# Making the low parts of two streamed weight slabs in one VectorE operation, in a two-block transformer kernel on one core

## The reference, cut to what matters

```python
h = rmsnorm(x, norm_g);  (... q, k, v, gates ...) = split_cols(h @ w_in, IN_SIZES)
merged = g_a * (oa @ w_up_a) + g_b * (ob @ w_up_b) + g_c * (oc @ w_up_c)
x = x + merged @ w_o
proj = rms_norm(h, g_pre_mix) @ w_in_2
m = sigmoid(gate_a) * (pool(proj) @ w_pool_out) + sigmoid(gate_b) * (conv(proj) @ w_conv_out)
h = h + rms_norm(m @ w_o_2, g_post_mix)
f = square(relu(rms_norm(h, g_pre_mlp) @ w_up_2)) @ w_down_2
h = h + rms_norm(f, g_post_mlp)
```

## Time and profile before

| | before |
|---|---|
| runs shown (3) | 2047.82, 2048.43, 2048.82 us |
| median | 2048.43 us |
| profiled execution, span from first to last instruction | 2046.3 us |
| own time of the profiled execution | not listed apart from its span |
| TensorE busy | 2034.2 us, 99% |
| TensorE weight loads | 1732.4 us, 85% |
| VectorE busy | 1358.7 us, 66% |
| ScalarE busy | 948.2 us, 46% |
| GpSimd busy | 80.7 us, 4% |
| low parts by rows, L487 | 438 operations, 540.2 us |
| DMA | 389.23 MB, mean 190 GB/s |

### The profile page before, as it was taken

The page is one execution under the profiler, slowest core; times in us unless marked ns, Lnnn a source line. Parts: engine busy times, 40 slices in busy tenths (PEclk is TensorE's granted clock), DMA queues, the critical chain, the costliest instruction groups (busy, mean ns, idle before and its releaser), DMA issues.

```text
span 2046.3 us, 29256 instructions
## 1 busy us (share of the span) xinstructions
PE 2034.2 (99%) x10572; PEld 1732.4 (85%) x10572; DVE 1358.7 (66%) x1815; ACT 948.2 (46%) x1225; POOL 80.7 (4%) x91
## 2 busy tenths in 40 slices
PE   9999999999999999999999999999999999999998
PEld 7888898888888888999888888888888888888886
DVE  6766756576756565678999756576556556645655
ACT  6645444565544444433444644553333333333343
POOL 0000102001011000002000000000000000000001
PEclk9999999999999999999999999999999999999999
DMA  9687555555566555555666565655565565555652
GB/s 348 196 199 189 176 155 182 183 168 180 185 217 220 192 188 187 171 175 158 193 194 200 181 232 185 196 171 189 194 189 185 194 195 181 196 191 184 194 195 103
DMA packets 265468, 389.23 MB, mean 190 GB/s; under 512 B 12504, under 2 KB 147032, under 8 KB 264571
## 3 DMA queue, kind: packets, MB, share of 16 engines
q1 hardware_dynamic: 262587, 377.19, 57.7%
q0 software_dynamic: 2624, 10.54, 2.0%
q10 hardware_dynamic: 144, 0.01, 0.0%
HBM read 385.02 MB, written 2.54 MB: 189 GB/s over the span
## 4 chain that ended last, share of the span: by engine, by line
PE 98%; SPq 1%; DMA 1%; DVE 0%; ACT 0%; issue 0%; DVEq 0%
PE acc L607 19%; PE acc L609 19%; PE acc L608 19%; PE acc L630 18%; PE acc L628 10%; PE acc L622 2%; PE acc L620 2%; PE acc L621 2%; PE acc L626 1%; PE aux L1489 1%; PE aux L1573 1%; DMA stage_rows<-in_w_mem_kv 1%; PE aux L1503 0%; PE acc L546 0%; PE acc L545 0%; PE acc L544 0%
## 5 line engine op out<-in xcount | busy, mean ns | idle before, releaser
L487 DVE TENSOR_TENSOR low_rows<-stage_rows,high_rows 128x1024 fp32r<-128x1024 f32 x438 | 540.2, 1237 | 404.1 <-ACT high_rows L476 399.2
L476 ACT ACTIVATE high_rows<-stage_rows 128x1024 fp32r<-128x1024 f32 x438 | 462.3, 1059 | 581.7 <-PE acc L609 531.0
L487 DVE TENSOR_TENSOR w_low<-stage,w_high 128x1024 fp32r<-128x1024 f32 (+1 forms) x264 | 320.7, 1221 | 230.8 <-ACT w_high L476 226.3
L476 ACT ACTIVATE w_high<-stage 128x1024 fp32r<-128x1024 f32 (+1 forms) x264 | 276.2, 1047 | 417.0 <-PE acc L630 298.9
L630 PE MATMUL acc<-u,w_high 128*128 128x512 f32 x900 | 247.9, 394 | 0.0
L607 PE MATMUL acc<-high_rows,f_pair 128*128 128x512 f32 x496 | 193.0, 389 | 0.0
L608 PE MATMUL acc<-low_rows,f_pair 128*128 128x512 f32 x496 | 192.9, 389 | 0.0
L609 PE MATMUL acc<-high_rows,f_pair 128*128 128x512 f32 x496 | 192.9, 389 | 0.0
L630 PE MATMUL acc<-hT,w_high 128*128 128x512 f32 x645 | 177.5, 394 | 0.0
L630 PEld LDWEIGHTS acc<-u,w_high 128*128 128x128 f32 x900 | 152.9, 189 | 19.0
L628 PEld LDWEIGHTS acc<-u,w_low 128*128 128x128 f32 x960 | 146.8, 188 | 20.6
(11 more groups left out here) (409 smaller groups left out, 3348.0 us busy)
## 6 DMA issues: line engine op xcount, KB each, us to landing
stage_rows<-in_w_in SPq DMA_DIRECT2D x160, 512.0 KB, 3.6
stage<-in_w_in SPq DMA_DIRECT2D x136, 512.0 KB, 3.5
stage_rows<-in_w_down SPq DMA_DIRECT2D x128, 512.0 KB, 4.3
stage<-in_w_up SPq DMA_DIRECT2D x120, 512.0 KB, 3.9
stage_rows<-in_w_o SPq DMA_DIRECT2D x64, 512.0 KB, 3.6
stage_rows<-in_w_pool_out SPq DMA_DIRECT2D x16, 512.0 KB, 3.8
stage_rows<-in_w_conv_out SPq DMA_DIRECT2D x16, 512.0 KB, 4.5
stage_rows<-in_w_mem_kv SPq DMA_DIRECT2D x14, 512.0 KB, 11.6
```

The source lines that it names most:

```text
L476: act.activation(high[:, pr, 0:kt, 0:p.cols], src[:, slot, 0:kt, 0:p.cols], ACT.Copy).then_inc(high_done, 1)
L487: dve.tensor_tensor(low[:, pr, 0:kt, 0:p.cols], src[:, slot, 0:kt, 0:p.cols], high[:, pr, 0:kt, 0:p.cols].bitcast(F32), ALU.subtract).then ...
```

## The change

Two helpers and a branch come into subtract_low. `two_tiles` says whether a slab is by rows with two tiles and not one of the first four of w_up_first. `in_couple` says whether slab n and its neighbour (n even: n+1, n odd: n-1) are both so. For a slab in such a couple the call for the even one issues nothing, and the call for the odd one waits until both are rounded and makes both low parts in one operation over two neighbouring places of each ring, 2048 columns. It then adds 2 to split_done. All others are made as before. ScalarE's rounding, the loads and TensorE's program are unchanged.

```diff
+        def two_tiles(n):
+
+            job, _, idx = stream_of_slabs[n]
+            p, _, _, kt, _ = job.pieces[idx]
+            return p.by_rows and kt == 2 and not (job is jobs["w_up_first"] and idx < 4)
+
+        def in_couple(n):
+
+            first = n - n % 2
+            return isinstance(n, int) and first + 1 < len(stream_of_slabs) and two_tiles(first) and two_tiles(first + 1)
+
         def subtract_low(dve, job, i, u, idx):
             n, n_static = job.slab(i, u, idx)
             p, _, k, kt, _ = job.pieces[idx]
             slot, pr = n_static % STAGES, n_static % PAIRS
+            if isinstance(n, int) and in_couple(n):
+                if n % 2:
+                    dve.wait_ge(high_done, n + 1)
+                    dve.tensor_tensor(low_rows[:, pr - 1:pr + 1], stage_rows[:, slot - 1:slot + 1],
+                                      high_rows[:, pr - 1:pr + 1].bitcast(F32), ALU.subtract).then_inc(split_done, 2)
+                return
             dve.wait_ge(high_done, n + 1)
```

## The result

| | before | after |
|---|---|---|
| runs | 2047.82 to 2048.82, four runs | 2059.78, 2060.67, 2062.17, 2064.82 |
| median | 2048.3 us | 2061.42 us |
| ratio, 95% interval | | 1.0067 [1.0054, 1.0080] |
| span of the profiled execution | 2046.3 us | 2057.7 us (its own time: 2059.78) |

The medians are 13.1 us apart.

The account below looks back on a forecast made before the run. TensorE, busy 2034.2 of 2046.3 us, was taken as the bound. mem_kv +3.6 and conv_gates with pool_out +4.2 gave +7.8 us, forecast 2056.2 us; the range ran from 2052.0 less 0.2 to 2064.

Parts of the forecast that it names:

- the 7 to 10 foretold: Sign expected in the changed kernel's profile: TensorE's waits for L487 low parts come to 7 to 10 us in all.
- The operation: VectorE's merged 2048-column operation takes 2294 ns; 209 couples save 180 ns each, 38 us busy time, priced at nothing.
- The spare time: Steady stages: the even slab's spare time before TensorE wants it falls from 5.6 to 1.7 us; nothing is lost.
- mem_kv: Term for the start: late couples (2, 3) and (8, 9) cost +3.6 us, the largest delay standing, not the sum.
- The first delay: In mem_kv, couple (2, 3) makes TensorE start slab 2 at 15.5 instead of 13.12: 2.4 us.
- the second delay: In mem_kv, couple (8, 9) makes slab 9 start at 37.25 instead of 33.46: 3.8 us for everything behind.
- Similar sums for w_up_a and w_up_c come out within half a us of nothing: Low-part readiness against TensorE's start in w_up_a and w_up_c: loss within half a us of nothing, left out.
- conv_gates and pool_out: Term of +4.2 us: delays add up, 0.7 at 338, 0.7 at 356, 1.8 at 390, 1.0 at 324.
- rival 2: TensorE's clock falls in one or both stalls at the start; two falls cost +4, about 2060 us; chance 0.10.
- Rival 1: Only the start is paid, TensorE not waiting at 338, 356 and 390: +3.6 us, 2052.0; chance 0.12.
- Rival 3: VectorE's backlog bites fully in conv_gates and pool_out, plus 2 us in w_down3: +15, about 2063 us; chance 0.18.
- Rivals 4 and 5: TensorE gains in conv_gates, at most 4 us, chance 0.03; the change does nothing anywhere, chance 0.01.

Follow-up runs that it names:

- experiments 3: Changed kernel with couples only in the steady stages (w_o, conv_out, w_o_2 and the w_down jobs; 98 couples): 2048.10 us, ratio 1.0001.
- 12: Changed kernel with 180 couples: none in mem_kv, at 320 to 334, 384 to 398, or at 156, 162, 208, 230, 338, 356; 2048.33 us.
- experiment 7: Couples only in the steady stages, plus an unused 1024-column subtraction ahead of each of 45 couples in w_down0 to w_down2: 2049.25 us, ratio 1.0007.
- experiment 8: Couples only in the steady stages, plus an unused 2048-column subtraction ahead of each of 45 couples in w_down0 to w_down2: 2071.31 us, ratio 1.0113.
- experiment 1: Changed kernel with couples in mem_kv alone (7 of the 209): 2051.02 us, ratio 1.0015.
- experiment 5: Changed kernel without couples in mem_kv, and in w_up_b the body runs ahead of the couple on VectorE: 2056.67 us, ratio 1.0042.
- Experiment 10: Changed kernel without couples in mem_kv, and with slabs 388 and 389 split singly: 2055.95 us, ratio 1.0039.
- 6: Changed kernel without couples in mem_kv, with 26 unused transposes on TensorE before its wait for slab 390: 2057.74 us, ratio 1.0046.
- 4: Changed kernel, but at the odd slab two operations of 1024 columns, each adding 1, in place of one of 2048: 2053.99 us, ratio 1.0028.
- 2: Changed kernel with all couples but those of mem_kv (202 of them): 2058.74 us, ratio 1.0054.
- 9: Changed kernel without couples in mem_kv and at eleven places late or one couple ahead of a late one (191 left): 2050.54 us, ratio 1.0013.
- 11: Changed kernel with 28 unused transposes on TensorE before its wait for slab 2: 2061.09 us, ratio 1.0065.

## Why the prediction was right, and where its sizes were off

Direction, mechanism and range held: slower, because the even slab's low part waits for the odd slab, at places where the spare time is short. Predicted +7.8 us, measured +11.4 in the span and +13.1 in the median. That the waits for low parts come to 8.3 us, within the 7 to 10 foretold, is in part luck: the forecast has two stalls of 2.7 us in mem_kv, the trace one of 3.7, and 2.9 at slab 390 where it has 1.8. Step by step:

- **The operation** (2.29 us, 209 couples, worth nothing): 2.31 us, 209, and by experiments 3 and 12 worth nothing. VectorE's busy time fell by 28 us to 1330.7 and not by 38; 209 x (2 x 1237 - 2308) ns is 35 us, and where the other 7 went wasn't looked at.
- **The spare time** (5.6 to 1.7 us): 1.6 by the timeline after (of 5.4, since the 5.6 leaves out the hand-over that the 1.7 has), over 1.2 by experiment 7 and 1.6 by 8. Steady stages lost nothing, and ScalarE waits for no load of weights behind mem_kv.
- **mem_kv** (+3.6): +2.2 in the profile, +3.2 by experiment 1. The first delay came as worked out (2.6 us, not 2.4), a fall of the clock put 1.5 on top, and the second delay, the one that was to set the stage's loss, didn't come: slab 9 started at 36.5 and not at 37.25. The step that failed is "31.00": the rounding of slab 9 was taken from one execution as fixed. It began 1.4 us sooner in after, and it began sooner in every other trace of this case too (29.3 to 30.9).
- **"Similar sums for w_up_a and w_up_c come out within half a us of nothing"**: the step with the largest miss. The part on the wait says that the body behind the couple comes 1.07 us later, but the sums compared only low parts with TensorE's start. w_up_b, which the text doesn't even name, lost 2.0 us by its body (experiment 5). w_up_c lost 0.8 by the couples themselves: the first is over at 491.59 us and TensorE starts slab 156 at 491.64. Each of its two delays, 0.45 and 0.35 us, is within the half us that was left out; together they are not.
- **conv_gates and pool_out** (+4.2): +6.3. 338 and 356 lost 0.7 each, as worked out. The 1.0 set for 324 appeared as 0.8 at its neighbour 322 and 0.15 at 324, so that its size is luck. Slab 390 lost 3.05, not 1.8: the sum took the rounding of 391 from the trace of before, where nothing had yet pushed it, while a couple two slabs ahead pushes it by its own length. Experiment 10 shows that.
- **The clock**, rival 2 with 0.10: it was a part of the truth, not an alternative to it. One fall in the profile of after, 1.5 us. Against it the prediction held that nothing in the trace shows a fall after a wait; the end of that trace does show one, though, without matmuls behind it: TensorE's last product is over at 2038.3 us, and the mean granted clock from 2041 to 2043 us is 0.56. The mean clock of the run of 2064.82 is 0.995 and that of 2059.78 is 0.998; 0.003 of 2058 us at half rate is 12 us, three or four falls more, and at 1.5 each that is about the 5 us between the two. This is an estimate from rounded means, and only one execution was profiled. One more fall in the middle runs would also cover the way from the profile's +11.4 to the median's +13.1; that isn't shown.
- **Rival 1** fell: 338, 356 and 390 waited. **Rival 3** set 9.2 us for conv_gates and pool_out, where 6.3 were measured; what is over the forecast there sits at 390 and not at 324 to 328, and nothing came of its 2 us beside GpSimd in w_down3. **Rivals 4 and 5** fell.

The sum with the measured terms: 2.2 + 2.8 + 6.3 + 0.2 = 11.5, the 11.4 of the span.

Why the clock falls behind one stall of 2.9 us and not behind the next stays open, and so does how often the start of the changed kernel pays its second delay, since each kernel has one profiled execution.

## What to carry to other kernels

Two operations merged into one hand over the first half as late as the second: price that not only for its own consumer but for all that stands behind the operation in the queue, and follow what you push back through the other engine to the next merged operation. In a stretch where the engine has a backlog, add the delay at the first hand-over that has no spare time, whichever it is. Busy time saved on an engine that nobody waits for is worth nothing, 26 us of it here.

## What was not expected of the hardware

- The granted clock fell to half for 3.4 us at single stalls of TensorE in an otherwise busy stream: at the start at stalls of 1.8 (experiment 7), 1.9 (6), 2.2 (8), 3.1 (4), 3.7 (after) and 4.6 us (1), at slab 390 at 2.9 us (2, 5), and at the second couples of w_down1 and w_down2 in experiment 8, at 1.8 us. In 1 and 2 it fell 0.6 and 0.4 us before the stall was over, elsewhere up to 1.5 us after. It did not fall at stalls of 1.5 (9, 10), 1.9 (12), 2.3 (3), at the second couple of w_down0 (1.8, in 8), at slab 390 at 1.8 us (4, 10) and 2.9 us (after, 11), and at slab 328 at 1.6 us (9). Each fall cost 1.3 to 1.7 us. None came where unused transposes filled the stall (6 at 390, 11 at slab 2), in one trace each.
- The changed kernel's four runs lie 5.0 us apart, where the larger groups of the kernel before (13 to 23 runs) have 1.9 to 2.4. Stalls alone don't make the scatter: the four runs of experiment 5, with the same stall of 2.9 us and a fall in its trace, lie within 0.25 us.
- Behind a stall the second matmul is late as well: in after the first two of slab 322 start at 978.26 and 978.60, 0.34 us apart where 0.23 is the rule, and those of slab 156 at 491.64 and 491.98. By the starts of slabs this 0.11 us shows at the next slab only (157, 163, 323). What does it wasn't tried.
